# Sine terms of the rotary step moved between partitions by DMAs and added on VectorE, in place of products with the identity and a turning matrix

## The chip, the cores and the metric

The kernel runs on one core of one Trainium2 chip. Its time is the device time of one execution in microseconds; lower is better. The median of three runs before the change is 997.94 us (997.82 to 999.81).

## The reference

Two network blocks run one after the other on an input of 256 tokens and 1024 features in float32. Each of the two layers of the first block mixes tokens in two ways: a gated recurrence (HGRN2, four heads of 128), and sparse attention (NSA, eight query heads and two key heads of 64) with a compressed, a selected and a window branch. The change is in the rotary embedding of the attention's queries and keys. It turns the first 16 of the 64 features of a head by an angle that depends on the token, and leaves the other 48 as they are:

```
def partial_rope(x, cos, sin):
    half = ROPE_DIM // 2
    x1, x2, xp = x[..., :half], x[..., half:ROPE_DIM], x[..., ROPE_DIM:]
    ...
    return jnp.concatenate([x1 * c - x2 * s, x1 * s + x2 * c, xp], axis=-1)
...
        qn = rmsnorm(heads(nq, NSA_HEADS), nsa_qnorm_g[i])
        q_nope = qn.reshape(B, KVH, G, T, dh)
        q_rope = partial_rope(qn, cos, sin).reshape(B, KVH, G, T, dh)
...
        k_sl = partial_rope(rmsnorm(heads(ksl, KVH), nsa_knorm_g[i, 1]), cos, sin)
        k_wn = partial_rope(rmsnorm(heads(kwn, KVH), nsa_knorm_g[i, 2]), cos, sin)
```

The rotated queries and keys feed only the scores of the selected and the window branch. The compressed branch takes the queries before the rotation.

## The kernel before

Activations lie with features on the 128 partitions and the 256 tokens along the free dimension, so two heads of 64 share a tile, and the rotation has to bring a value from another partition (8 rows up or down within a head). Each engine has its own program, written out by hand; they meet only through semaphores.

**Weights.** They stream through three slots of 1 MB panels (`load_panel`, L2790, issued by SyncE). A panel is split into a high and a low part before TensorE uses it: ScalarE casts the high part (`high_part`, L1377, tile panels_high), VectorE subtracts for the low part (`low_part`, L2004, tile panels_low), and each chunk of 128 output features then takes three products per input chunk (L483 to L485, 24 in a chunk). TensorE waits in `split(key)` until a panel's low part is there.

**Order in a layer.** TensorE's program is the written order. Between its large products stand small steps of the recurrence (`level(n, g)`, L784, eight levels of two halves, called by `some(2)`) and the gate projections, two chunks to a panel, taken one chunk at a time by `gate_chunk()` in the order hgo0, hgo1, hz0, hz1, nz0, nz1. The gate chunks after hgo0 all use PSUM bank 0, so the first chunk of a panel waits until ScalarE has copied the panel before it out of that bank. Each call of `todo(...)` on TensorE puts a step on an agenda; VectorE and ScalarE go through this agenda in its order and do their share of each step. After a step they also split panels, where `parts_out` and `in_units` allow it.

**The rotary step.** VectorE normalises the queries (L2315, tile q_nope) and keys (L2326, k_normed) and multiplies them by the tables cos and sin (L2319, tile squares, which is also called UW; L2330, tile k_rope_terms, also UK). TensorE forms the sum in PSUM: the identity times the cosine term plus the matrix `rot` times the sine term (L858 and L859 for the queries in two halves, L867 and L868 for the keys). ScalarE copies the queries to q_rope (step `copy qr0`, `copy qr1`) and the keys to k_padded (step `k_pad`, L1622 and L1623), from which the scores are formed (L688).

Of the kernel before, what the change touches and what calls it, by code (L numbers as in the profile page):

```python
# [8 lines left out]
P = 128  # L9
# [37 lines left out]
def const_table():  # L47
# [5 lines left out]
    rot = np.zeros((P, P))  # L53
    for h in (0, 64):
        for d in range(8):
            rot[h + 8 + d, h + d] = -1.0
            rot[h + d, h + 8 + d] = 1.0
    parts.append(("rot", rot))
# [3 lines left out]
    for h in (0, 8, 64, 72):  # L62
        cos[h:h + 8] = np.cos(ang.astype(np.float32))
        sin[h:h + 8] = np.sin(ang.astype(np.float32))
# [105 lines left out]
def build(nc, a, out):  # L170
# [4 lines left out]
    with ExitStack() as ctx:  # L175
# [197 lines left out]
        rope_ready, k_rope_ready = sem("q_rope_terms_ready"), sem("k_rope_terms_ready")  # L373
        blocks_ready = sem("cmp_blocks_ready")
# [50 lines left out]
        def _(pe):  # L425
# [317 lines left out]
            for l in range(DEPTH):  # L743
# [83 lines left out]
                todo(("q_norm",))  # L827
                pe.wait_ge(ksq_ready, l + 1)
                product(f"kss_{l}", 4, 512, head_ones, UK[:, 0:512])
                todo(("k_norm",))  # L830
                some(2)
# [23 lines left out]
                pe.wait_ge(rope_ready, l + 1)  # L855
                for j in range(2):
                    begin(f"qr{j}_{l}", 1 + j)
                    pe.matmul(ps[1 + j][:, :], ident, UW[:, j * 512:(j + 1) * 512], start=True, stop=False)  # L858
                    done(f"qr{j}_{l}", pe.matmul(ps[1 + j][:, :], const("rot"),  # L859
                                                 UW[:, 1024 + j * 512:1024 + (j + 1) * 512],  # L860
                                                 start=False, stop=True))
                    todo(("copy", f"qr{j}"))
                some(2)
                gate_chunk()
                pe.wait_ge(k_rope_ready, l + 1)
                begin(f"kr_{l}", 4)
                pe.matmul(ps[4][:, :], ident, UK[:, 0:512], start=True, stop=False)  # L867
                done(f"kr_{l}", pe.matmul(ps[4][:, :], const("rot"), UK[:, 512:1024], start=False, stop=True))  # L868
                todo(("k_pad",))
# [17 lines left out]
                todo(("cross",))  # L887
                gate_chunk()
# [34 lines left out]
                drained(pe, f"qr1_{l}")  # L923
                drained(pe, f"kr_{l}")
# [1966 lines left out]
```

## Time and profile before

| what | before |
|---|---|
| median of 3 runs | 997.94 us |
| the profiled execution: its own time | 1000.19 us |
| its span (first to last instruction) | 998.6 us |
| TensorE busy (matmuls) | 971.9 us (97%) |
| VectorE busy | 754.1 us (76%) |
| ScalarE busy | 618.5 us (62%) |
| GpSimd busy | 6.9 us (1%) |
| chain that ended last, by engine | PE 77%, DVE 12%, ACT 4%, issue 4%, DMA 2% |
| mean granted TensorE clock | 0.996 |

PE is TensorE, DVE VectorE, ACT ScalarE, POOL GpSimd, SP SyncE. The profiled execution took 1.6 us more than its span, and 2.25 us more than the median of the runs. The rotary step occurs once in each of the two layers of the first block. In the first it lies between 88 and 105 us of the span, in the second 204 us later with the same pattern. Times of instructions are their start in the span and their length. An engine's next instruction can start a little before the one ahead of it is counted as ended, so a run of instructions is best timed from start to start.

### The profile page before, as it was taken

How to read it: one execution, taken by the hardware profiler on the slowest of the kernel's cores; microseconds unless marked ns; L12 is line 12 of the kernel's file. 1: busy time of each engine (PE TensorE's matmuls, PEld its weight loads, DVE VectorE, ACT ScalarE, POOL GpSimd, SP SyncE). 2: the span in 40 equal slices, each digit the busy share in tenths (PEclk: the TensorE clock that was granted, in tenths of full speed). 3: DMA queues.
4: the chain of work that ended last, by engine and by line, in shares of the span. 5: the costliest groups of instructions: out<-in, count | busy, mean ns of one | idle time of the engine just before them, and what ended most of it. 6: DMA issues, size and time to landing. Idle time of an engine off the chain costs nothing.

```text
span 998.6 us, 18814 instructions
## 1 busy us (share of the span) xinstructions
PE 971.9 (97%) x7642; PEld 882.7 (88%) x7642; DVE 754.1 (76%) x1132; ACT 618.5 (62%) x918; POOL 6.9 (1%) x17
## 2 busy tenths in 40 slices
PE   7999999999999999999999999999998999999997
PEld 6997888998988889999998999999887998888886
DVE  7968676788576776897788777778786598868775
ACT  5744785676447765778466555557555576555564
POOL 2000000000000000000000000000000000000000
PEclk9999999999999999999999999999998999999999
DMA  9655513375637131836646565557272356655541
GB/s 304 201 160 165 175 57 113 107 231 163 176 114 234 43 127 44 293 104 199 190 152 206 181 204 170 202 174 220 88 257 81 104 164 201 207 182 196 172 164 43
DMA packets 143357, 164.00 MB, mean 164 GB/s; under 512 B 6302, under 2 KB 129832, under 8 KB 143288
## 3 DMA queue, kind: packets, MB, share of 16 engines
q1 hardware_dynamic: 142408, 161.97, 50.4%
q8 instruction: 51, 0.84, 0.3%
q10 hardware_dynamic: 464, 0.93, 0.2%
q0 software_dynamic: 416, 0.12, 0.1%
q14 instruction: 18, 0.15, 0.0%
HBM read 161.95 MB, written 1.05 MB: 163 GB/s over the span
## 4 chain that ended last, share of the span: by engine, by line
PE 77%; DVE 12%; ACT 4%; issue 4%; DMA 2%; SPq 0%; DVEq 0%; ACTq 0%
PE ps L483 16%; PE ps L484 15%; PE ps L485 15%; PE ps L1263 13%; PE ps L1261 7%; DVE panels_low L2004 4%; ACT panels_high L1377 2%; DVE squares L1967 1%; PE ps L501 1%; DVE input_parts L1963 1%; DMA panels<-in_w_in 1%; PE ps L593 1%; PE ps L784 1%; PE ps L688 1%; DVE neg_max L2038 1%
## 5 line engine op out<-in xcount | busy, mean ns | idle before, releaser
L2004 DVE TENSOR_TENSOR panels_low<-panels,panels_high 128x2048 fp32r<-128x2048 f32 (+1 forms) x145 | 327.5, 2262 | 94.3 <-ACT panels_high L1377 94.0
L1377 ACT CAST panels_high<-panels 128x2048 fp32r<-128x2048 f32 (+1 forms) x145 | 273.1, 1886 | 65.7 <-PE ps L485 41.0
L483 PE MATMUL ps<-input_parts,panels_low 128*128 128x256 f32 x832 | 241.5, 290 | 4.1 <-DVE input_parts L1999 2.1
L484 PE MATMUL ps<-input_parts,panels_high 128*128 128x256 f32 x832 | 235.2, 283 | 0.0
L485 PE MATMUL ps<-input_parts,panels_high 128*128 128x256 f32 x832 | 235.1, 283 | 0.0
L1263 PE MATMUL ps<-input_parts,panels_high 128*128 128x512 f32 x608 | 213.9, 395 | 0.0
L1261 PE MATMUL ps<-input_parts,panels_low 128*128 128x256 f32 x608 | 170.7, 281 | 0.7 <-DVE panels_low L2004 0.7
L483 PEld LDWEIGHTS ps<-input_parts,panels_low 128*128 128x128 f32 x832 | 159.1, 191 | 9.7 <-issue 3.8
L484 PEld LDWEIGHTS ps<-input_parts,panels_high 128*128 128x128 f32 x832 | 159.2, 191 | 0.6 <-issue 0.5
L485 PEld LDWEIGHTS ps<-input_parts,panels_high 128*128 128x128 f32 x832 | 159.2, 191 | 0.0
L1263 PEld LDWEIGHTS ps<-input_parts,panels_high 128*128 128x128 f32 x608 | 114.1, 188 | 26.3
L1261 PEld LDWEIGHTS ps<-input_parts,panels_low 128*128 128x128 f32 x608 | 114.8, 189 | 2.5 <-issue 1.3
L483 PE MATMUL ps<-ffn_hidden_high,panels_low 128*128 128x256 f32 x336 | 96.1, 286 | 1.7 <-issue 1.6
L485 PE MATMUL ps<-ffn_hidden_high,panels_high 128*128 128x256 f32 x336 | 95.2, 283 | 0.0
L484 PE MATMUL ps<-ffn_hidden_low,panels_high 128*128 128x256 f32 x304 | 85.7, 282 | 0.0
L483 PEld LDWEIGHTS ps<-ffn_hidden_high,panels_low 128*128 128x128 f32 x336 | 64.1, 191 | 2.9 <-issue 2.3
L485 PEld LDWEIGHTS ps<-ffn_hidden_high,panels_high 128*128 128x128 f32 x336 | 63.5, 189 | 0.0
L484 PEld LDWEIGHTS ps<-ffn_hidden_low,panels_high 128*128 128x128 f32 x304 | 57.2, 188 | 0.3
L1901 ACT CAST ffn_hidden_high<-values_hg 128x512 fp32r<-128x512 f32 x22 | 13.7, 621 | 58.4 <-DVE values_hg L2680 55.0
L1870 ACT COPY forget_key<-ps 128x512 f32<-128x512 f32 x36 | 21.0, 584 | 45.5 <-PE ps L1263 45.5
L483 PE MATMUL ps<-unscaled,panels_low 128*128 128x256 f32 x160 | 46.2, 289 | 0.0
L485 PE MATMUL ps<-unscaled,panels_high 128*128 128x256 f32 x160 | 45.3, 283 | 0.0
(342 smaller groups left out, 1625.8 us busy)
## 6 DMA issues: line engine op xcount, KB each, us to landing
panels<-in_ffn_up SPq DMA_DIRECT2D x44, 1024.0 KB, 5.1
panels<-in_w_in SPq DMA_DIRECT2D x29, 1024.0 KB, 5.6
panels<-in_ffn_down SPq DMA_DIRECT2D x22, 1024.0 KB, 4.8
panels<-in_mix_w_in SPq DMA_DIRECT2D x20, 1024.0 KB, 6.0
panels<-in_w_out SPq DMA_DIRECT2D x8, 1024.0 KB, 5.0
panels<-in_w_pg SPq DMA_DIRECT2D x8, 1024.0 KB, 5.1
panels<-in_mix_w_out SPq DMA_DIRECT2D x8, 1024.0 KB, 5.2
panels<-in_w_in SPq DMA_DIRECT2D x6, 512.0 KB, 5.7
```

The source lines that it names most:

```text
L483: pe.matmul(dst, w[1], x[0], start=start, stop=False if not kw else True, **kw)
L484: pe.matmul(dst, w[0], x[1], start=False, stop=False if not kw else True, **kw)
L485: return pe.matmul(dst, w[0], x[0], start=False, stop=stop, **kw)
L501: ins = pe.matmul(dst, w3[:, k, col:col + m], x3[:, k, :], start=(k == 0), stop=(k == nk - 1))
L593: done(name, pe.matmul(ps[b][:, 0:n], lhs, rhs, start=True, stop=True))
L688: ins = pe.matmul(ps[b + r][:, 0:2 * w].rearrange("p (k s) -> p k s", k=2), q[h, n * P:(n + 1) * P], keys[h, :, r, 0:w], start=False, stop ...
L1261: pe.matmul(both[:, 0, :], w_low, xh3[:, k, :], start=(k == 0), stop=True, skip_group_check=True)
L1263: ins = pe.matmul(both, w_high, x_parts[:, :, k, :], start=False, stop=True, skip_group_check=True)
L1377: nc.scalar.copy(high_slots[slot][:, 0:size], raw[n % SLOTS][:, 0:size]).then_inc(high_ready, 1)
L1870: nc.scalar.copy(sums[par][:, s, :], up_halves[half][:, :, 0, :]).then_inc(half_out, 1)
L1901: nc.scalar.copy(gh3[par], hidden[par]).then_inc(gh_ready, 1)
L2004: V.tensor_tensor(low_slots[slot][:, 0:size], raw[n % SLOTS][:, 0:size], high_slots[slot][:, 0:size].bitcast(F32), ALU.subtract).then_inc( ...
```

## The change

The identity and turning products are gone, with the matrix `rot` (64 KB of the constant table) and the two copies to q_rope. The sign of the turn goes into the table sin. After the multiplication by sin, GpSimd issues six DMAs for the queries and six for the keys in each layer, which write the sine term into q_rope and into k_normed, 8 rows lower or higher for the turned features, and in place for the other 48 rows of each head, where the term is zero. VectorE then adds the cosine and the sine term. ScalarE fills k_padded from this sum in SBUF.

The steps stand at other places too. On TensorE the key norm's product and `some(2)` come ahead of the step `q_norm`, so VectorE's level 6 comes ahead of the norms. The products with cos and sin form a step `rope_terms` of their own, behind level 7; the adds form the step `rope`, behind `cross`.

```
@@ const_table
-    rot = np.zeros((P, P))
...
-        sin[h:h + 8] = np.sin(ang.astype(np.float32))
+        sin[h:h + 8] = np.sin(ang.astype(np.float32)) * (-1 if h % 64 else 1)
@@ TensorE
-                todo(("q_norm",))
                 pe.wait_ge(ksq_ready, l + 1)
                 product(f"kss_{l}", 4, 512, head_ones, UK[:, 0:512])
+                some(2)
+                todo(("q_norm",))
                 todo(("k_norm",))
-                some(2)
...
-                pe.wait_ge(rope_ready, l + 1)
-                for j in range(2):
-                    begin(f"qr{j}_{l}", 1 + j)
-                    pe.matmul(ps[1 + j][:, :], ident, UW[:, j * 512:(j + 1) * 512], start=True, stop=False)
-                    done(f"qr{j}_{l}", pe.matmul(ps[1 + j][:, :], const("rot"),
-                                                 UW[:, 1024 + j * 512:1024 + (j + 1) * 512],
-                                                 start=False, stop=True))
-                    todo(("copy", f"qr{j}"))
                 some(2)
+                todo(("rope_terms",))
                 gate_chunk()
-                pe.wait_ge(k_rope_ready, l + 1)
-                begin(f"kr_{l}", 4)
-                pe.matmul(ps[4][:, :], ident, UK[:, 0:512], start=True, stop=False)
-                done(f"kr_{l}", pe.matmul(ps[4][:, :], const("rot"), UK[:, 512:1024], start=False, stop=True))
-                todo(("k_pad",))
...
                 todo(("cross",))
+                todo(("rope",))
                 gate_chunk()
...
-                drained(pe, f"qr1_{l}")
-                drained(pe, f"kr_{l}")
+                pe.wait_ge(q_roped, l + 1)
+                pe.wait_ge(kz_ready, l + 1)
@@ ScalarE
-                    elif step == "k_pad":
-                        full(act, name)
-                        src = v3(bank(name), 2)
+                    elif step == "rope":
+                        act.wait_ge(k_roped, l + 1)
+                        src = UK[:, 0:512].rearrange("p (k t) -> p k t", k=2)
...
                     elif step == "o_square":
...
+                        act.wait_ge(q_roped, l + 1)
@@ VectorE
+                    elif kind == "rope":
+
+                        dve.wait_ge(q_turned, 96 * (l + 1))
+                        V.tensor_tensor(QR[:, :], UW[:, 0:1024], QR[:, :], ALU.add).then_inc(q_roped, 1)
+                        dve.wait_ge(k_turned, 96 * (l + 1))
+                        V.tensor_tensor(UK[:, 0:512], UK[:, 0:512], KN[:, :], ALU.add).then_inc(k_roped, 1)
@@ GpSimd
+            turned_rows = [(h + 8, h, 8) for h in (0, 64)] + [(h, h + 8, 8) for h in (0, 64)] + \
+                          [(h + 16, h + 16, 48) for h in (0, 64)]
+
+            for l in range(DEPTH):
+                pool.wait_ge(rope_ready, l + 1)
+                for src, dst, n in turned_rows:
+                    pool.dma_start(QR[dst:dst + n, :], UW[src:src + n, 1024:2048]).then_inc(q_turned, 16)
+                pool.wait_ge(k_rope_ready, l + 1)
+                for src, dst, n in turned_rows:
+                    pool.dma_start(KN[dst:dst + n, :], UK[src:src + n, 512:1024]).then_inc(k_turned, 16)
```

VectorE's program before, first layer, from its reciprocal for the attention gates to the low part of panel hgo1 (the rows of level 6 and the hidden values shown in part):

```order
L2315 SCALAR_TENSOR_TENSOR q_nope<-q_nope,q_gain_scaled,gate_z 128x1024
L2319 TENSOR_TENSOR squares<-q_nope,consts 128x1024 x2
L2326 SCALAR_TENSOR_TENSOR k_normed<-k_normed,vectors,k_rope_terms 128x256 x2
L2330 TENSOR_TENSOR k_rope_terms<-k_normed,consts 128x512 x2
L2255 COPY decay_diag<-ps 32x4x32 x2
...
L2337 TENSOR_SCALAR small<-small 128x64
...
L2259 COPY decay_diag<-ps 64x4x64
...
L2004 TENSOR_TENSOR panels_low<-panels,panels_high 128x2048
```

The same place in the changed program, down to the adds. Level 6 is L2238 here, level 7 L2242, the hidden values L2327, and the low parts are L1987:

```order
L2238 COPY decay_diag<-ps 32x4x32 x2
...
L2298 SCALAR_TENSOR_TENSOR q_nope<-q_nope,q_gain_scaled,gate_z 128x1024
L2305 SCALAR_TENSOR_TENSOR k_normed<-k_normed,vectors,k_rope_terms 128x256 x2
L2327 TENSOR_SCALAR small<-small 128x64
...
L2242 COPY decay_diag<-ps 64x4x64
...
L2310 TENSOR_TENSOR squares<-q_nope,consts 128x1024 x2
L2314 TENSOR_TENSOR k_rope_terms<-k_normed,consts 128x512 x2
L1987 TENSOR_TENSOR panels_low<-panels,panels_high 128x2048
L2337 TENSOR_TENSOR cmp_values<-consts,ps 128x512
L1987 TENSOR_TENSOR panels_low<-panels,panels_high 128x2048 x2
L2344 SCALAR_TENSOR_TENSOR cmp_k_padded<-cmp_k,vectors,small 64x32 x2
L2321 TENSOR_TENSOR q_rope<-squares,q_rope 128x1024
L2323 TENSOR_TENSOR k_rope_terms<-k_rope_terms,k_normed 128x512
```

All the work that stood ahead of the low part of hgo1 still stands ahead of it, in another order: the products with cos and sin went from first to last. Two adds are new, behind two further low parts.

ScalarE's program in the changed kernel, first layer, from the copy of decay_cross (step `cross`) on. Before, the four k_padded copies stood some ten rows earlier and waited for a product in PSUM:

```order
L1353 COPY decay_cross<-ps 128x512 [waits psum_full7]
L1605 COPY k_padded<-k_rope_terms 64x2x256 [waits k_rope_ready]
L1606 COPY k_padded<-k_rope_terms 64x2x256
L1605 COPY k_padded<-k_rope_terms 64x2x256
L1606 COPY k_padded<-k_rope_terms 64x2x256
L1353 COPY gate_o<-ps 128x512 [waits psum_full0]
L1362 CAST panels_high<-panels 128x2048 [waits psum_full0,panel_landed0]
```

The four copies now wait for VectorE's second add, and the copy that empties PSUM bank 0 (gate_o, panel hgo1) stands behind them. (The printed wait k_rope_ready is the semaphore `k_roped`.)

## Rows read from the trace of the kernel before

**Rows 1.** Who TensorE waited for, 80 to 170 us: total, times, longest

```profile
PE ps L483 <- DVE input_parts L1999: 1.0, 1, 1.0
```

**Rows 2.** Chain that ended last, first layer: start us, us, what

```profile
87.33 0.59 PE ps L784 x29
...
93.14 0.94 PE ps L858 x2
...
96.66 1.07 PE ps L784 x16
...
99.11 0.12 PE ps L484
...
100.79 0.86 PE ps L867 x2
...
102.51 0.39 PE ps L593 x4
```

**Rows 3.** VectorE by time, first layer: start us, us, instruction, idle before

```profile
88.32 1.28 DVE L2315 SCALAR_TENSOR_TENSOR q_nope<-q_nope,q_gain_scaled,gate_z 128x1024 f32<-128x1024 f32 x1 [1.84 <-ACT gate_z L1363]
89.64 2.36 DVE L2319 TENSOR_TENSOR squares<-q_nope,consts 128x1024 f32<-128x1024 f32 x2
91.92 0.87 DVE L2326 SCALAR_TENSOR_TENSOR k_normed<-k_normed,vectors,k_rope_terms 128x256 f32<-128x256 f32 x2
92.83 1.29 DVE L2330 TENSOR_TENSOR k_rope_terms<-k_normed,consts 128x512 f32<-128x512 f32 x2
94.04 0.57 DVE L2255 COPY decay_diag<-ps 32x128 f32<-32x128 f32 x2
...
96.88 0.18 DVE L2337 TENSOR_SCALAR small<-small 128x64 f32<-128x64 f32 x1
...
98.09 0.41 DVE L2259 COPY decay_diag<-ps 64x256 f32<-64x256 f32 x1
...
100.09 2.27 DVE L2004 TENSOR_TENSOR panels_low<-panels,panels_high 128x2048 fp32r<-128x2048 f32 x1
102.94 0.69 DVE L2347 TENSOR_TENSOR cmp_values<-consts,ps 128x512 f32<-128x512 f32 x1 [0.57 <-PE ps L593]
103.54 2.28 DVE L2004 TENSOR_TENSOR panels_low<-panels,panels_high 128x2048 fp32r<-128x2048 f32 x1
```

**Rows 4.** TensorE by time: first products of panels hgo1 and hz0

```profile
102.71 0.36 PE L483 MATMUL ps<-input_parts,panels_low 128*128 128x256 f32 x1
...
112.55 0.36 PE L483 MATMUL ps<-input_parts,panels_low 128*128 128x256 f32 x1
```

**Rows 5.** ScalarE by time, first layer

```profile
93.18 0.22 ACT L1363 ACTIVATE small<-ps 128x64 f32<-128x64 f32 x1 [3.01 <-PE ps L850]
...
102.55 0.58 ACT L1622 COPY k_padded<-ps 64x512 f32<-64x512 f32 x1 [1.13 <-PE ps L868]
...
104.94 0.19 ACT L1368 COPY cmp_k<-ps 128x32 f32<-128x32 f32 x1
...
109.86 0.59 ACT L1368 COPY gate_o<-ps 128x512 f32<-128x512 f32 x1
```

**Rows 6.** TensorE's clock: core us, busy us (instructions) by engine, PEclk, DMA

```profile
758.00:760.00 2.00, 0.46 (x10) 0.23 (x5) 1.93 (x7) 2.00 (x8) 0.00 (x0) 1.00 0.00 0
760.00:762.00 2.00, 0.63 (x4) 0.40 (x4) 1.97 (x5) 1.49 (x2) 0.00 (x0) 0.74 0.00 0
...
766.00:768.00 2.00, 2.00 (x11) 1.58 (x8) 0.28 (x1) 0.00 (x0) 0.00 (x0) 0.56 0.00 0
```

**Rows 7.** TensorE by time near the program's start

```profile
12.52 0.41 PE L483 MATMUL ps<-ffn_hidden_high,panels_low 128*128 128x256 f32 x1
12.74 0.41 PE L484 MATMUL ps<-first_unscaled_low,panels_high 128*128 128x256 f32 x1
```

**Rows 8.** DMAs issued by GpSimd at the start (issue, then landing)

```profile
6.90 0.56 POOL L2756 DMA_DIRECT2D q_nope<-in_ffn_conv_w  x1
...
DMA to landing us min/median/max: 4.8/5.2/5.5
```

**Rows 9.** DMA issues by line: size, us to landing

```profile
out<-k_padded SPq DMA_DIRECT2D x1, 256.0 KB, 2.3
```

**Rows 10.** Three panel loads issued from 89.8 to 91.2 us

```profile
DMA to landing us min/median/max: 5.5/8.1/10.1
```

More of the change, by code:

```diff
@@ L51, in const_table @@
              ("head_ones", (p[:, None] // 64 == p[None, :] // 64).astype(float))]
-    rot = np.zeros((P, P))
[L54 to L58, printed above, removed]
     inv = (np.float32(500000.0) ** (-np.arange(0, 16, 2, dtype=np.float32) / np.float32(16))).astype(np.float32)
@@ L373, in build @@
         rope_ready, k_rope_ready = sem("q_rope_terms_ready"), sem("k_rope_terms_ready")
+        q_turned, k_turned = sem("q_sine_terms_moved"), sem("k_sine_terms_moved")
+        q_roped, k_roped, kz_ready = sem("q_rope_ready"), sem("k_rope_ready"), sem("k_padded_ready")
         blocks_ready = sem("cmp_blocks_ready")
@@ L1563, in _ @@
                 log_exp()
-                dest = {"nq0": QN[:, 0:512], "nq1": QN[:, 512:1024], "qr0": QR[:, 0:512], "qr1": QR[:, 512:1024],
-                        "ct": PCT[:, :], "hgo0": SG[:, 0:512], "hgo1": SG[:, 512:1024],
+                dest = {"nq0": QN[:, 0:512], "nq1": QN[:, 512:1024], "ct": PCT[:, :], "hgo0": SG[:, 0:512], "hgo1": SG[:, 512:1024],
                         "hz0": HZ[:, 0:512], "hz1": HZ[:, 512:1024], "nz0": NZ[:, 0:512], "nz1": NZ[:, 512:1024]}
@@ L1614, in _ @@
                         f(SS[:, 0:64], bank(f"hid_{l}")[:, 0:64], ACT.Exp, scale=-1.0).then_inc(hid_exp_ready, 1)
-                    elif step == "k_pad":
-                        name = f"kr_{l}"
-                        full(act, name)
-                        src = v3(bank(name), 2)
+                    elif step == "rope":
+                        act.wait_ge(k_roped, l + 1)
+                        src = UK[:, 0:512].rearrange("p (k t) -> p k t", k=2)
                         for g in range(2):
@@ L1623, in _ @@
                             ins = nc.scalar.copy(kz[64:128, :, 1, g, :], s)
-                        ins.then_inc(free(name), 1)
+                        ins.then_inc(kz_ready, 1)
                     elif step == "spread":
@@ L1645, in _ @@
                     elif step == "o_norm":
-                        act.wait_ge(rope_ready, l + 1)
                         head_rinv([f"oss{g}_{l}" for g in range(2)], UK[:, :], P, 1024).then_inc(o_rinv_ready, 1)
@@ L1669, in _ @@
                     in_units = (in_units or step == "scores") and step != "on"
-                    parts_out = (parts_out or step == "hidden_parts") and (step, *arg) != ("copy", "qr1")
+                    parts_out = (parts_out or step == "hidden_parts") and step != "rope_terms"
                     kv_in = kv_in or step == "cmp_kv"
@@ L2317, in _ @@
                         qn4 = v3(QN, 4)
-                        for i, tab in enumerate(("cos", "sin")):
-                            ins = V.tensor_tensor(UW[:, i * 1024:(i + 1) * 1024].rearrange("p (j t) -> p j t", j=4),
-                                                  qn4, const(tab).unsqueeze(1).to_broadcast([P, 4, T]), ALU.mult)
-                        ins.then_inc(rope_ready, 1)
                     elif kind == "k_norm":
@@ L2327, in _ @@
                                                         UK[:, 512 + j * T:512 + (j + 1) * T], ALU.mult, ALU.mult))
+                    elif kind == "rope_terms":
                         settle()
+                        for i, tab in enumerate(("cos", "sin")):
+                            ins = V.tensor_tensor(UW[:, i * 1024:(i + 1) * 1024].rearrange("p (j t) -> p j t", j=4),
+                                                  qn4, const(tab).unsqueeze(1).to_broadcast([P, 4, T]), ALU.mult)
+                        ins.then_inc(rope_ready, 1)
                         for i, tab in enumerate(("cos", "sin")):
@@ L2426, in _ @@
                         split_low(place, SPLIT_NO[("hgo0", l)])
-                    elif kind not in ("level", "k_pad") and (kind, *arg) != ("copy", "hz0") and not parts_out and (
+                    elif kind not in ("level", "rope_terms", "rope") and (kind, *arg) != ("copy", "hz0") and not parts_out and (
                             not in_units or kind == "scores" or (kind, *arg) == ("normalise", 7)):
```

## The prediction

> **What bounds the kernel now.** I read the list of TensorE's waits first, since the change takes work from TensorE and gives it to VectorE and the DMA queues. Between 80 and 170 us TensorE waited once, for 1.0 us [rows 1], so whatever TensorE does in this stretch is on the path. The chain of waits agrees: from 87 to 103 us it runs through TensorE alone, the rotary products included [rows 2]. Seen from there, taking products away looks like a gain of their full length. Next I read VectorE by time, because every panel that TensorE uses needs a low part from it. From 88.32 us, where it starts the query norm, to 102.36, where it ends the low part of hgo1 (100.09 + 2.27), it has no idle time at all [rows 3]. TensorE's first product with hgo1 stands at 102.71 [rows 4]. So VectorE, with 76% of the span busy on average, has about 0.3 us of slack at this one place: two engines are the bound here at once, and the change relieves one.
>
> **What the change takes from TensorE.** Query products: 93.14 to 96.66, 3.52 us. Key products: 100.79 to 102.51, 1.72 us [rows 2]. Together 5.24 us in a layer, 10.5 us in two. ScalarE loses two copies; it was waiting for TensorE around them, so nothing follows from this.
>
> **When TensorE can go on, and when VectorE lets it.** Without the products TensorE would be ready for hgo1 at 102.71 - 5.24 = 97.47. For VectorE I take the new order and the old lengths from start to start [rows 3]:
> - Level 6 no longer stands behind the norms. It needs TensorE's level products, which begin at 87.33 and whose first half is done 0.3 us on [rows 2]; with a hand-over I take 87.75. It lasts 96.88 - 94.04 = 2.84, to 90.6.
> - Query norm 1.32, key norm 0.91: to 92.8.
> - The hidden values need ScalarE's exponential, which starts at 93.18 when TensorE has made its input, and ends at 93.40 [rows 5]. TensorE is not earlier there in the changed program. VectorE waits some 0.6 us, starts at 93.45 and takes 98.09 - 96.88 = 1.21, to 94.66. It started the whole run 0.57 us earlier than before, and loses that here.
> - Level 7: 2.00, to 96.66. TensorE's products for it now follow directly at 93.1, so they are there.
> - Query terms 2.28, to 98.94; key terms 1.21, to 100.15.
> - Low part of hgo1: 2.27, to 102.42, against 102.36 before.
>
> So TensorE starts hgo1 at about 102.6, 0.1 us earlier than before, and stands still from 97.5 to 102.6. The 5.24 us do not arrive; they turn into a wait for VectorE. The work that VectorE was given less time for was never shortened, only sorted.
>
> **What comes behind.** VectorE does cmp_values (0.60) and the low parts of hz0 and hz1 (2.27 each), to 107.6; two small instructions for the compressed keys, for which I take 0.5 as an estimate (four of that kind take the 1.21 us above), to 108.1. The adds aren't in the trace; the terms are the same operation on the same sizes, 1.14 and 0.60 each, so the sum is ready at 109.85 if the DMAs have landed. ScalarE then copies k_padded: four copies took 104.94 - 102.55 = 2.39 [rows 5], and from SBUF I take the same. That ends at 112.3. Behind it in ScalarE's program stands the copy of hgo1 out of bank 0 (0.59), done at about 113.0; before, it started at 109.86 [rows 5]. TensorE wants this bank for hz0. Before, hz0 began at 112.55, 9.84 us after hgo1 [rows 4]; now TensorE would be there at 112.3 (some 0.2 us of those 9.84 were a wait for ScalarE, which is freer now). So with nothing else TensorE waits again, until 113.0: +0.45 us in a layer.
>
> **The DMAs.** GpSimd is idle, so its queue costs no other work. Twelve issues at 0.5 to 0.56 us [rows 8]: the queries' start at 99.0, the keys' six run from about 102.2 to 105.3, the last starting at 104.7. How long a move within SBUF takes the trace doesn't show. From below, 2.3 us for a store from SBUF in a quiet queue [rows 9]: 107.0. From above, GpSimd's loads at the start, 4.8 to 5.5 us beside full traffic [rows 8]: 110.2. The panel nz0 loads at the same time, but each of these moves is under 200 KB; I take 3.5, which is 108.2, ahead of the 109.2 at which VectorE has done the first add. The upper end would add 1.0 us. The queries' six start 2.7 us or more ahead, and VectorE wants them at 108.1, so even 5.5 us is enough. *DMA: Bandwidth & Descriptors* of the Trainium skill (Anatomy of one DMA) gives about 2.0 us fixed plus bytes over 436 GB/s for such a DMA; as an estimate that is 2.2 us for 96 KB, and nothing added, where the upper row adds 1.0.
>
> **TensorE's clock.** The new wait is long, and the trace has one place that is like it. From 758 to 762 us TensorE was busy 0.46 and 0.63 us of 2 each, and then the granted clock fell to 0.50, that is from 2.4 to 1.2 GHz; it was back at 1.00 inside 766 to 768 [rows 6]. 0.74 as the mean of 760 to 762 puts the fall near 761, 0.56 the rise near 767.8: 6.8 us. Here the stretch is 5.1 us with nothing in it, more idle than there, so I expect the fall in each layer. The price: at the low clock products of 256 columns follow at 0.22 us [rows 7], at the full one at 0.12 [rows 2], so a microsecond of low clock loses 0.45. Of 6.8 us, part falls into the wait itself. If it begins early in the wait, some 2 us are left behind 102.6, a loss of 0.9; if it begins at its end, all 6.8, a loss of 3.0. I take 4.5 us, a loss of 2.0. TensorE is then at hz0 at 112.3 + 2.0 = 114.3. The wait for bank 0 is covered by that: its own chain moves with the slow products by less (the compressed keys' norm hangs on TensorE) and comes to some 113.5. So the layer loses 114.3 - 112.55 = 1.7 us, bounds 0.6 and 2.7.
>
> **Sum.** Up to the start of hz0 a layer has -5.24 (products), +5.13 (wait for VectorE), -0.2 (wait for ScalarE gone), +2.0 (slow products): +1.7. Two layers make +3.4 us. Behind hz0 TensorE has next to no idle time [rows 1], so nothing there takes the delay back. The profiled execution would go from 1000.19 to 1003.6; against the median of the runs that is 997.94 + 3.4 = 1001.3 us.
>
> **The rivals.**
> - *The wait without the clock.* Everything as above, but the clock stays at full, since 5 us may fall otherwise than those at 758. Then the bank decides: +0.45 x 2 = +0.9 us, 998.8. For it: only one fall is in the trace. Against it: the idle stretch there was broken by work twice, and this one isn't.
> - *The moves land late.* In the range of panel loads that queue behind each other, 5.5 to 10.1 us [rows 10]. With 8.1 the keys' term lands at 112.8, VectorE's second add ends at 113.4, ScalarE's four copies at 115.9, the bank is free at 116.5: 4.0 us a layer, +8.0, 1005.9. It decides as soon as a move takes over 5.8 us, where the bank comes later than the slow products. Against it: there a megabyte each was queued, here the panels in flight are on another queue and one at a time. *SBUF — State Buffer* of the Trainium skill (SBUF: two separate sides) says that VectorE can lock GpSimd out of writing descriptors while it runs copies in its two-port mode; by it the operations here, all of two tensors, don't do that.
> - *The gain arrives.* TensorE gets hgo1 earlier than my order of VectorE's work has it, and the path keeps the products' 5.24 us in part. For that the low part of hgo1 must end before 102.0 or so, with the bank free as early; each microsecond there is one in the layer. If the whole wait vanished, -10.5: 987.5. For half of it VectorE would have to save 2.6 us of 14.7, and no row offers that; the exponential at 93.18 fixes what follows it. I put such a case at 992.7.
>
> **The numbers.** Chances: forecast 0.60, wait without the clock 0.19, late moves 0.13, gain 0.08. A difference of 0.2% (2.0 us) is about what a measurement of this kernel tells from none. The forecast runs from +1.2 to +5.4, a sixth of it under 2.0; with the second case that makes same 0.29, slower 0.50 + 0.13 = 0.63, faster 0.08. The range reaches from the second case less 0.3 us a layer for hand-overs that I rounded (998.2) to the forecast's upper end and a microsecond of the late moves (1004.4).
>
> **What would show it.** Right: in the changed trace TensorE is idle some 5 us in each layer, released by the low part of a panel; VectorE's terms end near 100.2 and that low part near 102.4 (times in the first layer); the granted clock falls to 0.50 behind it twice; the first add follows the compressed keys without a wait. Wrong: VectorE waits for a DMA at the adds; or TensorE's start on hgo1 is a microsecond or more before 102.6; or the clock stays at 1.00; or the copy out of bank 0 is what TensorE waits for at hz0.

## The result and the profile after

| what | before | after |
|---|---|---|
| median of 4 runs each | 997.88 us | 1006.05 us |
| the profiled execution: its own time | 1000.19 us | 1005.96 us |
| its span | 998.6 us | 1004.0 us |
| mean granted TensorE clock | 0.996 | 0.989 |

The ratio is 1.0066, with a 95% interval of 1.0051 to 1.0081: 6.6 us slower by the ratio, 8.2 by the medians, 5.8 by the profiles. In the second set of runs (5, beside 21 of before) the changed kernel was 4.7 us slower: 1003.73 us, ratio 1.0049 (1.0036 to 1.0063). The forecast was 1001.3, with 1004.4 as the upper end. The first medians lie far apart in part by chance: before has 999.04, 998.96 and 999.14 us in the three later sets of 17 to 23 runs, against 997.88 in the 4 of the first.

Three helpers moved up in the file: the low part of a panel is L1987 now (L2004 before), the first product of a chunk L479 (L483), the copy out of PSUM L1353 (L1368). In the experiments they move by a few lines again.

TensorE's waits, whole span of the changed kernel (total, times, longest):

```profile
PE ps L479 <- DVE panels_low L1987: 11.2, 6, 4.9
...
PE ps L479 <- ACT gate_o L1353: 1.8, 2, 1.4
```

TensorE by time in the changed kernel, the first products of hgo1 and hz0 in each layer, with the idle time ahead of them in brackets:

```profile
102.23 0.55 PE L479 MATMUL ps<-input_parts,panels_low 128*128 128x256 f32 x1 [4.88 <-DVE panels_low L1987]
...
115.97 0.39 PE L479 MATMUL ps<-input_parts,panels_low 128*128 128x256 f32 x1 [1.43 <-ACT gate_o L1353]
...
310.05 0.55 PE L479 MATMUL ps<-input_parts,panels_low 128*128 128x256 f32 x1 [4.88 <-DVE panels_low L1987]
...
322.89 0.39 PE L479 MATMUL ps<-input_parts,panels_low 128*128 128x256 f32 x1 [0.35 <-ACT gate_o L1353]
```

Two of the six waits for a low part are new and last 4.9 us: they take the place of the products. The product with hgo1 starts 0.48 us earlier than in [rows 4], but hz0 starts 3.42 us later. In the second layer hz0 is 6.30 us later than before, where it stood here:

```profile
316.59 0.36 PE L483 MATMUL ps<-input_parts,panels_low 128*128 128x256 f32 x1
```

In the first layer something between the two takes 3.90 us more. Two things show. Here is the clock (us, length, then busy time of PE, weight loads, DVE, ACT and POOL, the granted clock, DMA share, GB/s):

```profile
98.00:100.00 2.00, 0.00 (x0) 0.00 (x0) 2.00 (x4) 2.00 (x3) 1.03 (x3) 1.00 1.03 331
100.00:102.00 2.00, 0.00 (x0) 0.00 (x0) 2.00 (x1) 1.06 (x4) 2.00 (x5) 0.78 0.47 76
102.00:104.00 2.00, 1.77 (x8) 1.80 (x9) 2.00 (x3) 1.24 (x1) 2.00 (x5) 0.50 0.80 176
104.00:106.00 2.00, 2.00 (x12) 2.00 (x11) 2.00 (x2) 0.00 (x0) 1.06 (x3) 0.50 0.92 273
106.00:108.00 2.00, 2.00 (x11) 2.00 (x11) 1.09 (x1) 0.00 (x1) 0.00 (x0) 0.52 0.98 253
108.00:110.00 2.00, 2.00 (x18) 2.00 (x19) 1.38 (x3) 1.94 (x6) 0.00 (x0) 1.00 1.07 300
```

After TensorE had done nothing from 98 us on, the granted clock fell to 0.50, from 2.4 to 1.2 GHz. The mean of 0.78 over 100 to 102 us puts the fall near 101.1, a microsecond before its work came back, and the 0.52 over 106 to 108 puts the rise near 107.9. So the low spell lasts 6.8 us, of which 5.7 lie on products: 11 or 12 in two microseconds where 18 fit at 1.00. The other is VectorE and ScalarE by time:

```profile
98.60 1.28 DVE L2314 TENSOR_TENSOR k_rope_terms<-k_normed,consts 128x512 f32<-128x512 f32 x2
99.81 2.28 DVE L1987 TENSOR_TENSOR panels_low<-panels,panels_high 128x2048 fp32r<-128x2048 f32 x1
...
109.12 1.23 DVE L2321 TENSOR_TENSOR q_rope<-squares,q_rope 128x1024 f32<-128x1024 f32 x1
112.08 0.69 DVE L2323 TENSOR_TENSOR k_rope_terms<-k_rope_terms,k_normed 128x512 f32<-128x512 f32 x1 [1.73 <-DMA k_normed<-k_rope_terms]
```

```profile
112.81 0.62 ACT L1605 COPY k_padded<-k_rope_terms 64x512 f32<-64x512 f32 x1 [2.11 <-DVE k_rope_terms L2323]
...
115.33 0.58 ACT L1353 COPY gate_o<-ps 128x512 f32<-128x512 f32 x1
```

The second add waits 1.7 us for the keys' moves. Behind it stand four copies of 0.62 us, then the copy that empties bank 0, and then TensorE at hz0 (115.97). The summary of the moves of the keys in the first layer:

```profile
L2757 POOL DMA_DIRECT2D k_normed<-k_rope_terms x6: 502/518/538, 102.0 to 104.5; - x6
...
DMA to landing us min/median/max: 4.8/5.5/7.5
```

By size, over both layers (KB each, median us to landing):

```profile
k_normed<-k_rope_terms POOLq DMA_DIRECT2D x4, 96.0 KB, 6.2
k_normed<-k_rope_terms POOLq DMA_DIRECT2D x8, 16.0 KB, 5.2
```

### The profile page after: what moved, and what is told of

Same layout as the page of the kernel before. It is cut to its first block, busy times and chain, and to the rows that moved or that the text cites. A ratio compares the mean times of both kernels' runs of the same rounds, so it can differ in the third digit from the quotient of the medians.

```text
span 1004.0 us, 18788 instructions
## 1 busy us (share of the span) xinstructions
PE 966.1 (96%) x7618; PEld 883.6 (88%) x7618; DVE 758.0 (76%) x1136; ACT 617.0 (61%) x914; POOL 19.0 (2%) x41
## 4 chain that ended last, share of the span: by engine, by line
PE 75%; DVE 13%; ACT 4%; issue 4%; DMA 3%; POOL 1%; SPq 0%; DVEq 0%; POOLq 0%; ACTq 0%
PE ps L479 16%; PE ps L480 15%; PE ps L481 15%; PE ps L1248 13%; PE ps L1246 7%; DVE panels_low L1987 4%; ACT panels_high L1362 2%; DVE squares L1950 1%; DMA k_normed<-k_rope_terms 1%; PE ps L497 1%; DVE input_parts L1946 1%; DMA panels<-in_w_in 1%; PE ps L589 1%; PE ps L684 1%; DVE neg_max L2021 1%
## 5 line engine op out<-in xcount | busy, mean ns | idle before, releaser
L1987 DVE TENSOR_TENSOR panels_low<-panels,panels_high 128x2048 fp32r<-128x2048 f32 (+1 forms) x145 | 327.3, 2261 | 94.9 <-ACT panels_high L1362 94.8
L479 PE MATMUL ps<-input_parts,panels_low 128*128 128x256 f32 x832 | 243.8, 293 | 15.1 <-DVE panels_low L1987 10.6
L479 PEld LDWEIGHTS ps<-input_parts,panels_low 128*128 128x128 f32 x832 | 161.2, 194 | 21.2 <-issue 13.0
L480 PEld LDWEIGHTS ps<-input_parts,panels_high 128*128 128x128 f32 x832 | 161.5, 194 | 0.7 <-issue 0.5
L481 PEld LDWEIGHTS ps<-input_parts,panels_high 128*128 128x128 f32 x832 | 161.4, 194 | 0.0
L1248 PEld LDWEIGHTS ps<-input_parts,panels_high 128*128 128x128 f32 x608 | 114.0, 188 | 26.0
L479 PE MATMUL ps<-ffn_hidden_high,panels_low 128*128 128x256 f32 x336 | 95.9, 286 | 2.2 <-issue 1.6
L479 PEld LDWEIGHTS ps<-ffn_hidden_high,panels_low 128*128 128x128 f32 x336 | 64.1, 191 | 3.1 <-issue 2.3
L479 PE MATMUL ps<-unscaled,panels_low 128*128 128x256 f32 x160 | 46.2, 289 | 0.0
```

Source lines behind the costliest of these rows:

```text
L479: pe.matmul(dst, w[1], x[0], start=start, stop=False if not kw else True, **kw)
L480: pe.matmul(dst, w[0], x[1], start=False, stop=False if not kw else True, **kw)
L481: return pe.matmul(dst, w[0], x[0], start=False, stop=stop, **kw)
L1248: ins = pe.matmul(both, w_high, x_parts[:, :, k, :], start=False, stop=True, skip_group_check=True)
L1987: V.tensor_tensor(low_slots[slot][:, 0:size], raw[n % SLOTS][:, 0:size], high_slots[slot][:, 0:size].bitcast(F32), ALU.subtract).then_inc( ...
```

## The experiments

Each is set against the changed kernel as it measured in the second set, 1003.73 us; ratios are to the kernel before as it ran beside each. "The clock's low spell" is the time at a granted clock of 0.50, worked out from the means of two-microsecond windows as above.

**The changed kernel again.**

> The changed kernel, unchanged, as the measure for the three below and for the open part of its difference: the profile of the changed kernel is 5.8 us above the profile of before, the medians differ by 8.2 us. If the profiles tell all, the median lies 5 to 6 us above before (1003 to 1004). If some executions lose more than the profiled one, it stays at 7 to 9 us above.

1003.73 us (1002.29 to 1004.33). Its profile has hgo1 and hz0 within 0.25 us of the first one's in both layers, so the rotary step costs the same, yet its own time is 1003.62 where the other's is 1005.96. The difference is at another place. The first profile, then the second, over the same work:

```profile
766.00:768.00 2.00, 0.58 (x5) 0.34 (x4) 1.97 (x5) 1.25 (x2) 0.00 (x0) 0.68 0.00 0
768.00:770.00 2.00, 2.00 (x10) 1.32 (x12) 1.10 (x2) 1.41 (x3) 0.00 (x0) 0.50 0.00 0
```

```profile
766.00:768.00 2.00, 0.58 (x6) 0.34 (x5) 1.97 (x5) 1.20 (x2) 0.00 (x0) 1.00 0.00 0
768.00:770.00 2.00, 2.00 (x22) 1.64 (x20) 1.05 (x2) 1.45 (x3) 0.00 (x0) 1.00 0.00 0
```

The fall of [rows 6] comes in some executions and not in others, with the same idle time ahead of it, and is worth the 2.3 us by which the spans differ. The profile of before has it too, so it is no part of the 5.8 us between the first profiles. It may be a part of the 8.2 us between the first medians; that isn't settled.

**Filler products in the wait.**

```
                 product(f"vc_{l}", 3, 64, HIDV[:, :], W2[:, P:P + 64])
                 todo(("cmp_kv",))
+                pe.wait_ge(psum_free[1], bank_fills[1])
+                for _ in range(5):
+                    pe.matmul(ps[1][:, :], ident, CN[:, 0:512], start=True, stop=True)
```

> TensorE gets five products of 512 columns (results unused, bank 1) in the 4.9 us in which it waits for the low part of hgo1, once in each layer; everything else stays. Both theories say that the granted clock then stays at 1.00 behind the wait. Theory A (two holds that overlap: the slow products, and behind them the late key moves through the bank): the first add's and the second add's times are set by the moves, so bank 0 comes free when it did, TensorE is earlier there and waits longer, some 3.8 us instead of 1.4 in the first layer and 3.0 instead of 0.35 in the second; the time moves by less than 1 us against the changed kernel. Theory B (the two losses add up): 2.6 and 2.9 us of slow products are gone and the waits at hz0 stay as they are, 5.5 us faster than the changed kernel.

1007.62 us (ratio 1.0088, 1.0074 to 1.0102): 3.9 us slower than the changed kernel, which neither theory had. The clock stayed at 1.00 behind the wait for hgo1, and TensorE was early at hz0 and waited there, as A has it:

```profile
116.09 0.58 PE L479 MATMUL ps<-input_parts,panels_low 128*128 128x256 f32 x1 [4.00 <-ACT gate_o L1356]
...
325.24 0.39 PE L479 MATMUL ps<-input_parts,panels_low 128*128 128x256 f32 x1 [3.04 <-ACT gate_o L1356]
```

In the first layer hz0 stands where it stood (115.97): the bank held the path, and the slow products had been hidden by it. What A missed is the next window: the long wait at hz0 brings its own fall.

```profile
112.00:114.00 2.00, 0.09 (x1) 0.00 (x0) 0.69 (x1) 1.06 (x2) 0.00 (x0) 1.00 1.10 349
114.00:116.00 2.00, 0.00 (x0) 0.00 (x0) 0.00 (x0) 1.95 (x4) 0.00 (x0) 0.57 0.56 185
116.00:118.00 2.00, 1.91 (x9) 1.92 (x10) 0.01 (x1) 1.98 (x3) 0.00 (x0) 0.50 0.06 19
118.00:120.00 2.00, 2.00 (x11) 2.00 (x11) 2.00 (x1) 1.97 (x3) 0.00 (x0) 0.50 0.00 0
```

In the changed kernel the fall overlapped with the hold; here it comes behind it, and both are paid.

**k_padded filled later.**

```
                 todo(("o_square",))
+                todo(("pad",))
...
-                    elif step == "rope":
+                    elif step == "pad":
```

> ScalarE fills k_padded one step later, behind its share of the step o_square, so its copy of hgo1 out of bank 0 no longer waits for VectorE's second add; nothing else changes. Theory A: the waits for bank 0 at hz0 (1.4 us and 0.35 us in the changed kernel's profile) go, the slow products stay: 1.8 us faster than the changed kernel, both clock falls still there. Rival: ScalarE's work that is moved back comes late for something else (the square of the recurrence's output, or the scores that need k_padded), and the gain is 0.

1000.07 us (1.0012, 1.0003 to 1.0021): 3.7 us faster than the changed kernel, where 1.8 was expected. TensorE doesn't wait at hz0 in either layer (114.04 and 319.19). At the first that is 1.9 us earlier, of which 1.43 are the wait. The rest of the gain lies with the clock, which this edit doesn't touch: behind the same 4.9 us of waiting the low spell began near 100.1 in the first layer, so that more of it fell into the wait, and in the second it lasted 3.4 us instead of 6.8. So of the 3.7 us the waits account for 1.8, as expected. Whether the rest is chance or something that the edit does to the clock, this run doesn't tell.

**Both.**

> Both edits: filler products in the wait for hgo1, and k_padded filled later. Theory A: neither hold is left, hz0 starts some 9.7 us after hgo1, near 112.0 us in the first layer instead of 115.97, and 3.0 us earlier in the second: 7 us faster than the changed kernel, about the time of before (within 1.5 us). Theory B (losses that add up): 1.8 + 5.5 = 7.3 us too, so this run does not tell A from B by itself but the sum of e1 and e2 against it does: by A it is more than twice their sum, by B it is their sum.

998.26 us (0.9995, 0.9985 to 1.0005), the time of before. The filler alone gave +3.9, the late copies alone -3.7, both -5.5 (A had 7): the effects don't add. hgo1 to hz0 takes 9.54 us (the same in the second layer):

```profile
102.24 0.36 PE L479 MATMUL ps<-input_parts,panels_low 128*128 128x256 f32 x1 [0.53 <-DVE panels_low L1992]
...
111.78 0.36 PE L479 MATMUL ps<-input_parts,panels_low 128*128 128x256 f32 x1
```

This is the clean length, against which the changed kernel's 12.31 and 12.49 us (13.74 and 12.84 less the waits of 1.43 and 0.35) give the slow products: 2.8 and 2.95 us. It also shows that the change as it stands frees nothing: with both new costs gone it is even with before, since the 4.9 us are still spent, only on unused products.

**The old order of steps with the moves.**

```
@@ VectorE: cos and sin products again right behind their norms
@@ TensorE
                 todo(("q_norm",))
                 pe.wait_ge(ksq_ready, l + 1)
                 product(f"kss_{l}", 4, 512, head_ones, UK[:, 0:512])
                 todo(("k_norm",))
                 some(2)
```

> DMAs and adds of the changed kernel, but the steps of before's order: on TensorE and VectorE the query norm with its cos and sin products, then level 6, then the key norm with its products, stand where they stood before the change. VectorE's work ahead of the low part of hgo1 is the same, so TensorE's wait for it stays near 4.9 us and the clock falls behind it. What changes is when the moves start: the queries' about 5 us earlier, and the keys' before 102 us. Theory (the late keys hold bank 0): no wait at the second add, none at hz0, 1.8 us or a little more faster than the changed kernel, 1001 to 1002. Rival (the moves are slow wherever they stand, because panel loads fill the DMA engines): the second add waits as before and nothing is gained.

1007.94 us (1.0082, 1.0069 to 1.0095), 4.2 us slower than the changed kernel, which neither the theory nor the rival had. The wait for hgo1, which was to stay, is gone and comes back at four places: 2.4 and 0.8 us for level 6, 2.4 for ScalarE's copy of the cross blocks, 2.2 for bank 0. Issued from 91.9 to 98.0, the moves lie across the panel loads:

```profile
98.00:100.00 2.00, 2.00 (x12) 2.00 (x11) 2.00 (x7) 0.69 (x1) 0.00 (x0) 0.50 1.11 218
100.00:102.00 2.00, 2.00 (x17) 2.00 (x16) 1.97 (x1) 1.35 (x2) 0.00 (x0) 0.86 1.05 186
```

```profile
107.01 1.91 ACT L1362 CAST panels_high<-panels 128x2048 fp32r<-128x2048 f32 x1 [4.21 <-DMA panels<-in_w_in]
```

The DMA engines are full (a share above 1) and move 186 to 218 GB/s; in the changed kernel the same share carries 350 GB/s at 94 to 96 us, where panels are alone. The panel lands late and ScalarE stands 4.2 us for it. VectorE's low part of that panel waits for the cast:

```profile
108.95 2.29 DVE L1987 TENSOR_TENSOR panels_low<-panels,panels_high 128x2048 fp32r<-128x2048 f32 x1 [3.79 <-ACT panels_high L1362]
```

The second add had no wait for its moves, as the theory had it, but comes at 112.83 by this, and the bank's copy is in line behind.

**The keys' moves from ScalarE's queue.**

```
+                        act.wait_ge(k_rope_ready, l + 1)
+                        for src, dst, n in ...:
+                            act.dma_start(KN[dst:dst + n, :], UK[src:src + n, 512:1024]).then_inc(k_turned, 16)
```

> The six key moves are issued by ScalarE in its step cmp_kv, where it waits for TensorE anyway, instead of by GpSimd behind the queries' six. They can start at about 99.8 us and need no 3 us of issue on GpSimd. Theory (GpSimd's serial issue of 12 DMAs, 0.5 us each, makes the keys late): they land by 106, the second add doesn't wait, bank 0 comes free near 114.0: 1.8 us faster than the changed kernel. Rival (the panel load in the DMA engines makes them late): they land after 109 and the wait stays, or ScalarE's waiting for the key terms delays its panel casts, and the kernel is no faster.

1003.34 us (1.0045), no change. The second add came 0.36 us earlier (111.72) and still waited 0.5 us. The issue is no cheaper on ScalarE, 4.8 us for six, and holds its next cast:

```profile
100.46 4.77 ACTq L1624 DMA_DIRECT2D k_normed<-k_rope_terms  x6
105.33 1.90 ACT L1362 CAST panels_high<-panels 128x2048 fp32r<-128x2048 f32 x1 [4.65 <-issue]
```

So the theory of GpSimd's serial issue is not really tested: ScalarE began 1.5 us earlier, but ended its issue 0.2 us later than GpSimd had. What the run shows is that ScalarE's queue is no way round it.

**No zero rows moved.**

```
-            turned_rows = [(h + 8, h, 8) ...] + [(h, h + 8, 8) ...] + [(h + 16, h + 16, 48) for h in (0, 64)]
+            turned_rows = [(h + 8, h, 8) ...] + [(h, h + 8, 8) ...]
```

> This kernel leaves out the two moves of 48 rows in each set, which write the zeros of the sine term; the sums in those rows then take what the tiles held. Only the four moves of 8 rows are left in each set, 16 KB or 32 KB each. Theory (issue): the keys' last issue starts 2 us earlier and the last to land is a small one; the second add doesn't wait and the time falls by 1.8 us against the changed kernel. Rival (panel loads): the small moves land as late as the large, 7 us after their issue, and the wait shrinks by the 2 us of issue at most.

This kernel leaves the zeros out, so its result is not the reference's. 1000.05 us (1.0013, 1.0003 to 1.0022): 3.7 us faster than the changed kernel, with no wait at the adds and none at hz0. The groups of DMA issues (times, KB each, median us to landing):

```profile
q_rope<-squares POOLq DMA_DIRECT2D x8, 32.0 KB, 2.0
k_normed<-k_rope_terms POOLq DMA_DIRECT2D x8, 16.0 KB, 1.9
```

The same 16 KB moves took 5.2 us in the changed kernel. Two things changed at once here: the bytes, and the place. The keys' four went out from 100.9 to 102.9, three of them ahead of the panel load asked for at 102.1, and the slowest of the four took 4.7 us. So both theories hold a part: a move ahead of the panel takes 2 us, one beside it more, and with fewer moves fewer fall beside it. A part of the gain in this profile is the clock's again: the waits for hgo1 are the same 4.87 us, but the low spell lasts 3.4 us in each layer instead of 6.8, and hgo1 to hz0 takes 10.9 and 10.8 us, 1.4 and 1.3 over the clean 9.54. First layer:

```profile
100.00:102.00 2.00, 0.00 (x0) 0.00 (x0) 2.00 (x2) 1.20 (x4) 2.00 (x5) 0.98 0.47 76
102.00:104.00 2.00, 1.79 (x8) 1.82 (x9) 2.00 (x3) 1.14 (x1) 0.91 (x2) 0.50 0.44 83
104.00:106.00 2.00, 2.00 (x14) 2.00 (x13) 2.00 (x2) 0.00 (x0) 0.00 (x0) 0.67 1.06 370
```

**Zeros by GpSimd.** The same, but GpSimd writes the zeros, and the result is the reference's again:

```
+                pool.wait_ge(k_rinv_ready, l + 1)
+                nc.gpsimd.memset(QR[:, :], 0.0).then_inc(q_zeroed, 1)
                 pool.wait_ge(rope_ready, l + 1)
+                pool.wait_ge(q_zeroed, l + 1)
...
                 pool.wait_ge(k_rope_ready, l + 1)
+                nc.gpsimd.memset(KN[:, :], 0.0).then_inc(k_zeroed, 1)
+                pool.wait_ge(k_zeroed, l + 1)
```

> The result stays the reference's here: instead of the moves of 48 rows, GpSimd sets q_rope (before the terms are there) and k_normed (behind the queries' four moves) to zero, and only the eight moves of 8 rows a layer are left, 192 KB of 768. Theory (the bytes of the zeros make the key moves late and take the DMA engines): the same as the run that left the zeros out, 1000 us within 1 us, the key moves landed before the first add, no wait at hz0. Rival (filling on GpSimd disturbs VectorE or delays the issue): VectorE's norms or terms get longer by 0.5 us or more and the time stays at 1002 or above.

1000.43 us (1.0007, 0.9998 to 1.0016), as the theory has it. VectorE's norms and terms keep their lengths, and the second add follows the first at 110.48 without a wait. The low spells are 6.8 us in both layers, as in the changed kernel, so this run is the forecast's own case, with the moves on time. It is 3.3 us faster than the changed kernel, and hz0 starts without a wait:

```profile
114.73 0.36 PE L480 MATMUL ps<-input_parts,panels_low 128*128 128x256 f32 x1
...
320.37 0.36 PE L480 MATMUL ps<-input_parts,panels_low 128*128 128x256 f32 x1
```

That is 2.2 and 3.8 us later than before, where the forecast had 1.7 and 3.4. The panels asked for at 102 to 107 us were slow as well. The changed kernel, then this one (min, median, max):

```profile
DMA to landing us min/median/max: 10.2/10.3/10.8
```

```profile
DMA to landing us min/median/max: 5.8/6.6/7.3
```

The kernel before has 5.5 there. So the moves nearly doubled the panels' landing, from 5.5 to 10.3 us, and most of that were the zeros. It cost nothing that the trace shows: ScalarE's waits for panels between 95 and 135 us add up to 3.6 us in both. The keys' moves, issued at 102.0 to 103.5 beside the panels, took 4.4 us in the median here against 5.5, and the last of them left earlier. *DMA: Bandwidth & Descriptors* of the Trainium skill (Queues, rings and completion order) says that a DMA engine takes its queues in turn, a packet from each; the trace agrees so far as moves and panels both got slower when they met.

**Low part first.**

```
                     elif kind == "rope_terms":
+                        split_low(place, SPLIT_NO[("hgo1", l)] + 1)
                         settle()
```

with k_padded late as above.

> VectorE makes the low part of hgo1 ahead of the rope_terms step (3.5 us of products with cos and sin), and k_padded is filled one step later as in the second experiment; the moves and the adds start up to 2.3 us later. Theory (the products' 5.2 us a layer are there, and the order on VectorE turns them into a wait): the low part ends near 98.7, TensorE waits 1.4 us instead of 4.9, the clock does not fall, hz0 starts near 108.5 instead of 116.0: 7 us a layer, some 12 to 14 us faster than the changed kernel, 990 to 992. Rival (VectorE is the bound of the stretch whatever the order): the 3.5 us come back as waits of TensorE for the low parts of hz0 or nz0 or for the compressed keys, with the time of the filler version, near 998.

994.88 us (0.9952, 0.9939 to 0.9966): 8.9 us faster than the changed kernel and 4.1 faster than before. hz0 starts at 108.71 as expected. The missing 3 to 5 us: TensorE waits 1.6 and 1.9 us for hgo1, and the clock fell in the second layer all the same; and the keys' moves landed so late (the second add waited 4.1 us) that ScalarE's copies came behind and cost TensorE 0.4 and 0.8 us at the scores.

**Low part first, zeros by GpSimd, k_padded where the change has it.**

> The kernel of the run above with the low part of hgo1 ahead of the terms on VectorE, and k_padded filled where the changed kernel does it, ahead of the copy out of bank 0. Theory (bank 0 is the next hold, whatever the moves do, since the adds come behind the low parts of hz0 and hz1): ScalarE's copy of hgo1 can't start before 111.5, TensorE is at hz0 near 108.5, waits 3 to 3.5 us in each layer, and the clock may fall behind it: 6 to 10 us slower than the version below. Rival (with the moves on time the bank is no hold): no wait at hz0 and the time of the version below.

1006.89 us (1.0076, 1.0063 to 1.0089). The bank is the next hold whatever the moves do, and it brings the fall:

```profile
114.99 0.58 PE L480 MATMUL ps<-input_parts,panels_low 128*128 128x256 f32 x1 [4.31 <-ACT gate_o L1354]
```

```profile
112.00:114.00 2.00, 0.00 (x0) 0.00 (x0) 0.00 (x0) 1.97 (x4) 0.00 (x0) 0.90 0.66 208
114.00:116.00 2.00, 1.01 (x4) 1.01 (x5) 0.00 (x0) 1.95 (x3) 0.00 (x0) 0.50 0.00 0
```

In the second layer the wait is 5.5 us. Against the next run, which differs only in where ScalarE makes four copies, that is 14.6 us, more than the 6 to 10 expected.

**All three.**

> Low part of hgo1 first, k_padded later, zeros by GpSimd. Against the version without the last of these (994.9 us, which still had a wait of 4.1 us for the key moves on VectorE, and 0.4 us of TensorE for ScalarE's norm at 118.6): theory (VectorE's wait is off the path there): 0 to 1 us faster, 994 to 995. Rival (moves still cost by slowing the panels): 2 us faster or more, 993 or below.

992.31 us (0.9933, 0.9918 to 0.9948), faster than both kernels: 6.8 us under before. Against the version that moves the zeros it is 2.6 us by the medians, 1.9 by the ratios, whose intervals overlap a little, so the rival (2 us or more) is likely right but not by much. Of the late landings the cost is seen: the two waits at the scores, 1.2 us, are gone. That slow panels cost something is not shown. What is left of the stretch is 1.7 and 1.8 us for the low part of hgo1:

```profile
98.96 0.36 PE L480 MATMUL ps<-input_parts,panels_low 128*128 128x256 f32 x1 [1.69 <-DVE panels_low L1990]
...
299.55 0.53 PE L480 MATMUL ps<-input_parts,panels_low 128*128 128x256 f32 x1 [1.79 <-DVE panels_low L1990]
```

**The old order, zeros by GpSimd.**

> The order of steps of before with the DMAs and adds, as in the third experiment (1007.9 us), with zeros by GpSimd. Theory (that kernel was 4 us slower than the changed one since its moves, issued from 91.9 to 98.0, lie across three panel loads and made the panel after them late, with waits of ScalarE's cast of 4.2 us): with a quarter of the bytes the panels come in time and the time falls by 4 us or more, to 1001 to 1004; the waits of 3.2 us for level 6 stay. Rival (the old order itself is the loss): it stays within 1.5 us of 1007.9.

1001.22 us (1.0023, 1.0014 to 1.0032), 6.7 us faster than with the zeros moved, and within 1 us of the new order. The waits for level 6 are still there (3.2 and 2.8 us), and the fall too, now behind that wait (0.50 from 96 to 102 us). The wait for bank 0 is down from 2.2 to 1.0 us in each layer. The panels of the stretch land in 5.3 us again instead of 7.7. So both orders cost about as much, and what made the old one bad were the bytes.

## Why the prediction was right or wrong

- **Products gone, wait for VectorE in their place: right.** Expected 5.1 us until 102.6; measured 4.88 us until 102.23, with this run 0.33 us earlier at the exponential of [rows 5]. The order on VectorE was as worked out from [rows 3]: terms 2.3 and 1.2 us, the low part directly behind. The low-first version shows it by undoing it: with the low part ahead of the terms, hz0 starts 7.3 us earlier.
- **The clock: right as a mechanism, too small.** 2.0 us was taken, of bounds 0.9 and 3.0; measured 2.8 and 2.95. The length of the low spell, 6.8 us, was right. The step put 4.5 us of it behind the wait, and 5.7 and 6.1 fell there, since the fall began only 1.1 and 0.7 us before the end of the wait. That looks like chance more than error: in the run with k_padded later the fall came 2.5 us before the end, and the loss was 1.9.
- **The key moves: wrong, and the step whose mechanism failed.** "Each of these moves is under 200 KB; I take 3.5", upper bound 5.5; measured up to 7.5. The small size was no protection: beside panels even 16 KB took 4.4 us with the zeros gone. And the step counted each move by itself, not that the twelve carry 768 KB a layer, three quarters of a panel more than before, 576 KB of it zeros, into DMA engines that are 80 to 98% busy from 102 to 108 us. [rows 9], the quiet queue, was the wrong neighbour. The rival of late moves, given 0.13, had the mechanism and the place, and its price, a microsecond for each over 5.8, fits: 7.5 - 5.8 = 1.7, against a wait of 1.43. That its total, 1005.9 us, is near the first median is luck: it took 8.1 us for a move and 8.0 for the two layers, where hz0 shows 6.3. Two of the signs named for being wrong came: VectorE waits for a DMA at the second add, and TensorE for bank 0 at hz0. With the zeros taken out of the moves both go, and hz0 of the second layer is 3.8 us late instead of 6.3, near the forecast's 3.4.
- **The bank covered by the slow products: wrong in consequence.** It was to be free at 113.5 with TensorE there at 114.3. It was free at 115.9. In the second layer the moves took 6.6 us at most and the wait was 0.35.
- **The sum.** Up to hz0 the first layer was to lose 1.7 us and lost 3.42: -0.48 at hgo1, +2.8 slow products, +1.43 bank, -0.3 for the small wait that went. The second lost 2.88 more (316.59 before, 322.89 after), 6.3 in all against 3.4 predicted. Of these 2.9 us too much, the bank is 1.8, which the prediction put at nothing, and the clock 1.7; the early start at hgo1 and smaller terms took back some 0.6. So the late moves are only about half of what was missed. The span grew by 5.4: some 0.9 us came back later, at a place that I did not find. The medians differ by 8.2 and 4.7 us in the two sets; the median of the second lies below the forecast's upper end, that of the first above it, and what tells the two apart is open. So is this: the three versions that lose the wait for bank 0 and keep the one for hgo1 at 4.9 us (k_padded later, no zero rows, zeros by GpSimd) are 3.3 to 3.7 us faster than the changed kernel by their medians, twice the 1.8 us of its waits at hz0. In their profiles a shorter or earlier low spell makes up much of the rest; no run shows why.
- **The gain that didn't arrive.** The rival said that VectorE would have to save 2.6 of 14.7 us and that no row offers that. No work had to be saved; it was enough that 3.5 us of it, not needed by anybody yet, stood behind the low part. The prediction had the rows for this but looked only at the order given.

## What to carry to other kernels

When work is taken off the engine on the path, look at which engine it meets next, and put what that engine owes it ahead of what nobody waits for: the same operations took 1003.7 or 992.3 us by their order and by who wrote the zeros. Count the bytes of small DMAs against the stream that already fills the DMA engines, and move only the rows that change. A wait removed can uncover a second one behind it that is dearer, since its fall of the clock no longer hides in the first: remove them together, and test them together.

## What the runs showed of the hardware

- Moves of 16 KB within SBUF landed in about 2 us ahead of a panel load, in 4.4 beside one, and in 6.0 across several (the last experiment). For the 96 KB moves of the changed kernel the median was 6.2 us, where the estimate in the prediction from *DMA: Bandwidth & Descriptors* of the Trainium skill (Anatomy of one DMA) is 2.2; the measurement decides. With the larger moves among the panels (the old order), full DMA engines carried 186 to 218 GB/s, against 350 with panels alone. Why these bytes are dearer was not tried.
- Six DMA issues took 3.0 us on GpSimd and 4.8 us on ScalarE.
- The granted clock fell to 0.50 in or just behind waits of 2.4 to 5.5 us with TensorE idle, but also around some of under 2 us. Of the waits for the low part of hgo1 in the three versions with the low part first, those of 1.56, 1.69 and 1.71 us had no fall, and those of 1.78, 1.79 and 1.89 had one. Six waits make no rule. At 766 us the same stretch had a fall in one execution and not in another.
- The low spells behind the wait of 4.9 us lasted 6.8 us in some profiles and 3.4 in others, with the same wait ahead. From hgo1 to hz0 a spell of 6.8 cost 1.9 to 2.95 us, by how much of it lay in the wait, and one of 3.4 cost 1.3 to 1.5. So one profile tells what a fall costs there, not how often it comes or how long it lasts, and versions that differ by a microsecond or two have to be compared by their medians, and with the spells read beside them.
